# A decoder step on one core: differential heads moved two ahead, their logits in pieces over two PSUM bank pairs, scalings moved to ScalarE, and the first norm put inside the input projection

## The reference, cut to what matters

```
xn  = rmsnorm(x, norm_mix)
qa, ka, va, qi, ki, wi, qb, kb, vb = split(xn @ w_in)      # 2628 columns
qa, ka, qb, kb = rmsnorm over each head of 64              # with their gains
A = attention of qa over the 256 keys chosen by qi, ki, wi # top-k per token
B: for each of 4 heads, causal:
   p_c = softmax(qb_c @ kb_c^T / 8 + bias)   for c = 0, 1
   o   = (p_0 - lam * p_1) @ vb
   out = rmsnorm(o, diff_subln) * (1 - lam_init)
h  = x + concat(A, B) @ w_out
h2 = h + memory attention;   y = h2 + conv FFN
```

## Time and profile before

| | |
|---|---|
| time, median of 3 runs | 2556.97 us (2551.84 to 2562.08) |
| the profiled execution | 2553.21 us, its span 2551.4 us |
| PE busy | 2322.0 us, 91% |
| DVE busy | 1103.8 us, 43% |
| ACT busy | 673.3 us, 26% |
| POOL busy | 678.4 us, 27% |
| first norm | 0 to 33.2 us (start of the first projection matmul); its last square ends at 19.3 us |
| input projection | 33.2 to 418.2 us; a step of 512 columns takes 7.3 us, one of 324 columns 5.7 us |
| differential heads | 418.2 to 593.8 us |
| everything after | 598.3 to 2551.4 us, not touched |

### The profile page before, as it was taken

One profiled execution on the slowest core, in us unless ns is written; L12 is line 12 of the kernel. 1 busy time (PEld: TensorE's weight loads), 2 busy tenths in 40 slices (PEclk: granted clock), 3 DMA queues, 4 the chain that ended last, 5 costly groups with the idle time before them and its releaser, 6 DMA issues. The chain is left out here.

```text
span 2551.4 us, 32464 instructions
## 1 busy us (share of the span) xinstructions
PE 2322.0 (91%) x12441; PEld 1564.4 (61%) x12461; DVE 1103.8 (43%) x2457; ACT 673.3 (26%) x1713; POOL 678.4 (27%) x722
## 2 busy tenths in 40 slices
PE   6999997886888888888889898989999999999999
PEld 4644443563455555555544345458888888888887
DVE  4469997883355443333413112243433433370001
ACT  2321112452455444544501014311111111100000
POOL 1021131112455455567700010021212222201110
PEclk9999998997999999998999899999999999999999
DMA  3211101004699698876730204101111111122221
GB/s 136 73 64 67 47 1 41 1 1 149 222 337 316 240 317 308 299 241 195 202 151 1 82 0 165 66 36 49 36 51 34 51 34 51 34 72 74 71 64 39
DMA packets 148605, 281.74 MB, mean 110 GB/s; under 512 B 14485, under 2 KB 83780, under 8 KB 148452
## 3 DMA queue, kind: packets, MB, share of 16 engines
q0 software_dynamic: 49408, 176.19, 20.6%
q1 hardware_dynamic: 80756, 90.50, 10.7%
q10 hardware_dynamic: 18288, 12.98, 1.7%
HBM read 261.68 MB, written 17.94 MB: 110 GB/s over the span
## 5 line engine op out<-in xcount | busy, mean ns | idle before, releaser
L607 PE MATMUL PS<-region 128*128 128x512 f32 (+5 forms) x864 | 331.7, 539 | 4.3 <-DMA region<-w_in 4.3
L2569 PE MATMUL PS<-region,ffn_w 128*128 128x264 f32 x1408 | 323.3, 389 | 1.6 <-PEq L2020 1.6
L2569 PEld LDWEIGHTS PS<-region,ffn_w 128*128 128x128 f32 x1408 | 269.4, 191 | 48.5 <-issue 2.0
L607 PEld LDWEIGHTS PS<-region 128*128 128x128 f32 (+1 forms) x864 | 155.2, 184 | 166.8 <-issue 140.5
L2569 PE MATMUL PS<-region,side 128*128 128x264 f32 x1056 | 243.3, 387 | 1.6 <-POOL side L2526 1.6
L1801 ACT COPY region<-PS 128x512 f32<-128x512 f32 x352 | 193.0, 593 | 183.8 <-PE PS L1680 90.3
L2569 PEld LDWEIGHTS PS<-region,side 128*128 128x128 f32 x1056 | 198.9, 190 | 35.0 <-POOL side L2526 1.7
L851 DVE TENSOR_SCALAR_CACHE_REDUCE mask<-score,cand 128x384 bf16<-128x384 f32 (+2 forms) x198 | 181.6, 942 | 3.3
L1680 PE MATMUL PS<-ident_f,region 128*128 128x128 f32 x1024 | 141.5, 281 | 23.7 <-ACT region L1801 21.5
L1550 POOL DMA_INDIRECT region<-cache_b_k,gather_b x128 | 121.2, 947 | 138.0 <-PE PS L1680 114.4
L1550 POOL DMA_INDIRECT region<-cache_b_v,gather_b x128 | 122.4, 956 | 90.1 <-PE PS L1763 56.1
(11 more groups left out here) (423 smaller groups left out, 3808.7 us busy)
## 6 DMA issues: line engine op xcount, KB each, us to landing
ffn_w<-w_gate SPq DMA_DIRECT2D x11, 1024.0 KB, 5.4
ffn_w<-w_up SPq DMA_DIRECT2D x11, 1024.0 KB, 5.4
region<-w_in SPq DMA_DIRECT2D x4, 2048.0 KB, 7.8
ffn_w<-w_down ACTq DMA_DIRECT2D x7, 704.0 KB, 5.4
region<-x_prompt ACTq DMA_DIRECT2D x8, 512.0 KB, 7.5
region<-x_prompt SPq DMA_DIRECT2D x8, 512.0 KB, 10.5
mem_keys<-cache_mem_k SPq DMA_DIRECT2D x8, 512.0 KB, 4.2
mem_values<-cache_mem_v SPq DMA_DIRECT2D x8, 512.0 KB, 9.3
```

Of the source, the lines that this page charges most:

```text
L607: last = nc.tensor.matmul(M.PS[0:n, s % 3, 0:chunks[j].width], XT[:, c, t * P:t * P + n], w[j % 2][:, c, 0:chunks[j].width], start=(c == 0 ...
L2569: last = nc.tensor.matmul(M.PS[:, bank, 0:TW], left[:, c, :], right[:, c, :], start=begin and c == 0, stop=(c == KH - 1), skip_group_check ...
```

## The change

1. **First norm inside the projection.** `norm_transpose_stage` becomes a class `FirstNorm` whose parts are called from the projection's block. TensorE turns tiles 0 to 4 before step 0, then one more tile ahead of each of steps 1 to 4; the squares go to PSUM banks 6 and 7, one bank per half tile, not doubled, and the scaled rows to the space of `KTB`. The four pieces of the first weights wait for the scaling of tiles 0 to 3 alone, the second chunk's weights for tile 7.
2. **Scalings of the projection by ScalarE.** In the three chunks with a norm over 512 columns the multiplication by the reciprocal root is done by ScalarE, one activation for each of 8 heads; the keys' gains by GpSimd. `room(s)` counts one VectorE operation there instead of two or three.
3. **Differential heads.** Logits, maxima and exponentials run two heads ahead. Heads of up to 512 keys are one piece, longer ones two pieces of half the keys; piece g uses banks 0-1 or 2-3 (g % 2), one branch in each bank. A maximum takes both branches in one instruction; with two pieces a minimum joins them, and an addition the sums. The output scaling moves from VectorE to ScalarE, without the gain, which becomes a scale of the "M" copy (a column `sub`, loaded by one more transfer of `first_loads`). TensorE's order is `logits(n + 2)`, `transposes(n)`, `values(n - 1)`.

```diff
+    def dve(self, eng, s):                       # FirstNorm
+        if s == 0:
+            self.setup.columns(eng)
+            self.scale(eng, 0)
+        for t in range(self.copied, min(NT, s + self.AHEAD + 1)):     # AHEAD = 4
+            if t + 1 < NT:
+                self.scale(eng, t + 1)
+            for b in range(2):
+                eng.wait_ge(self.tr_done, 2 * t + b + 1)
+                nc.vector.tensor_tensor(M.XT[...], M.PS[:, 6 + b, 0:4 * n] ..., ALU.mult
+                    ).then_inc(self.evac_done, 1)
+    def pe(self, eng, s):
+        for t in range(self.turned, min(NT, s + self.AHEAD + 1)):
+            eng.wait_ge(self.scaled, t + 1)
+            for b in range(2):
+                if t:
+                    eng.wait_ge(self.evac_done, 2 * t - 1 + b)
+                for c in range(4):
+                    last = nc.tensor.transpose(M.PS[:, 6 + b, c * n:(c + 1) * n], ...)
+                last.then_inc(self.tr_done, 1)
+        if s == 0:
+            eng.wait_ge(self.sq_done, NT)
+        if s < NT:
+            eng.wait_ge(self.evac_done, 2 * s + 2)
...
                         for x, first in enumerate(w_first):
+                            if first_norm:
+                                sp.wait_ge(first_norm.scaled, x + 1)
...
+                def normalise(s):                # projection, ScalarE, after the sides of step s
+                    act.wait_ge(rstd_done, normed(s + 1))
+                    for h in range(cols // hd):
+                        last = nc.scalar.activation(dst, M.PS[0:n, s % 3, h * hd:(h + 1) * hd], ACT.Copy,
+                                                    scale=rstd[0:n, s % 2, h:h + 1])
+                    last.then_inc(nat_mul, 1)
...
-                    ops = 2 + (len(c.gains(0, P, 0)) if c.gains else 0)
+                    ops = 1 if by_scalar(s) else 2 + (len(c.gains(0, P, 0)) if c.gains else 0)
...
-        def slot(k, a, b):                       # differential heads
-            return M.PS[:, 2 * k:2 * k + 2, :].rearrange("p b n -> p (b n)")[:, a:b]
+        def pieces(n):
+            nk = (heads[n][0] + 1) * P
+            return [(0, nk)] if nk <= CH else [(0, nk // 2), (nk // 2, nk)]
+        def slot(g, w):
+            return M.PS[:, 2 * (g % 2):2 * (g % 2) + 2, 0:w]
...
+                    for x, (a, b) in enumerate(pieces(n)):
+                        g = piece0[n] + x
+                        if g >= 2:
+                            pe.wait_ge(s_used, 2 * (g - 1))
...
+                for what, n in order:            # ScalarE
+                    if what == "B" and n + 2 < N:
+                        exps(n + 2)
+                    ...copies(n)
+                    if n:
+                        square(n - 1)
+                    if n >= 2:
+                        outputs(n - 2)
...
                                                    ALU.add).then_inc(comb_done, 1)
-                    if n + 1 < N:
-                        maxima(n + 1)
-                    if n:
-                        outputs(n - 1)
+                    if n + 2 < N:
+                        maxima(n + 2)
                     M.top.rounds(link, share)
```

More of the change, by code:

```diff
@@ L403, in dve @@
                                                  K(f"new_mask{g}"), ALU.add))
[L406 to L415, removed]
-            "sq_done", "ms_done", "rstd_done", "scaled", "tr_done", "evac_done"))
[L417 to L482, removed]
-                    for c in range(KC):
-                        last = nc.tensor.transpose(M.PS[:, 2 * (t % 2) + c // 4, (c % 4) * n:(c % 4 + 1) * n],
-                                                   xs[0:n, t % 2, c * P:(c + 1) * P], K("ident")[0:n, 0:n])
-                    last.then_inc(tr_done, 1)
@@ L503, in projection_stage @@
     turned = lambda s: count(s, lambda c: c.sources is not None)
+    counted = lambda s: count(s, lambda c: c.gains is not None)
+    by_scalar = lambda s: bool(beside and chunks[steps[s][0]].norm and chunks[steps[s][0]].norm[0] > 2 * P)
     def stored(s):
@@ L554, in load @@
                         return
+                    if j == 1 and first_norm:
+                        sp.wait_ge(first_norm.scaled, NB)
                     sp.dma_start(w[j % 2][:, :, 0:c.width],
@@ L672, in _ @@
                                             ALU.pow).then_inc(rstd_done, 1)
+                    if c.gains is not None and by_scalar(s):
+                        pool.wait_ge(nat_mul, k)
+                        if s >= 2 and turned(s - 1):
+                            pool.wait_ge(tr_done, turned(s - 1))
+                        if s >= 2 and stored(s - 2):
+                            pool.wait_ge(store_done[s % 2], stored(s - 2))
+                        for dst, a, b in c.gains(t, n, s % 2):
+                            last = nc.gpsimd.tensor_tensor(dst, a, b, ALU.mult)
+                        last.then_inc(nat_done, 1)
             @block.vector
@@ L729, in _ @@
                         side.dve(dve, s, room(s))
-                    if chunks[j].norm:
+                    if chunks[j].norm and not by_scalar(s):
                         normalise(s, k)
@@ L1039, in prompt_differential_stage @@
     N = len(heads)
-    turn_after = {min(B_H * (i + 1) + 1, N - 1): i for i in range(NB - 1)}
+    turn_after = {min(B_H * (i + 1) + 2, N - 1): i for i in range(NB - 1)}
     order = []
@@ L1134, in _ @@
                 logits(0)
+                logits(1)
                 for what, n in order:
-                    if what == "B" and n + 1 < N:
-                        logits(n + 1)
+                    if what == "B" and n + 2 < N:
+                        logits(n + 2)
                     transposes(what, n)
-                    if what == "B":
+                    if what == "B" and n:
+                        values(n - 1)
+                    if what == "B" and n == N - 1:
                         values(n)
```

229 lines of the change are left out of this document (164 added, 65 removed).

## The result

The changed kernel takes 2540.32 us (median of 20 runs, 2530.39 to 2555.25), the one before 2556.91 us (20 runs, 2551.84 to 2565.81): ratio 0.9939, 95% interval 0.9927 to 0.9951, so 0.6% faster. I had forecast 2522, and 2506 to 2540. The direction was right; the gain is 16.6 us where I had some 35 against this median (33.5 in the sum of the parts). The profiled execution took 2537.3 us (span 2535.5), so its difference of 15.9 us to the span before can be taken apart, each stage from one trace.

What follows compares the result with a forecast made beforehand. TensorE (91% busy) was taken to bound, gains coming from its gaps at start, projection end and heads. Gains 9.0 + 1.7 + 13.8 + 6.0 + 3 = 33.5 us from 2553.2 give 2519.7; forecast 2522, range 2506 to 2540.

Steps and rivals of the forecast that it cites:

- First norm: Projection start: TensorE begins step 0 at about 22.6 instead of 33.2; net gain 9.0 us, bounds 5 and 12.
- So it is hidden: Projection start: the first weights' last piece lands by 24, before its matmuls need it at 26, so costs nothing.
- Scalings: Projection: ScalarE's scaling no longer waits behind VectorE's search at the end; gain 1.7 us, bounds 0 and 2.8.
- rival (c): Projection: ScalarE bounds it, its chain exceeding 7.3 us a step, so the kernel gets slower, 2570 us; chance 0.04.
- Heads up to 512 keys: Differential stage, 16 short heads: two ahead leaves no ring of one head; gain 13.8 us, bounds 5 and 20.
- Heads over 512 keys: Differential stage, 16 long heads: a shorter ring, 6.4 against 6.85 us at 1024 keys; gain 6.0 us, bounds 0 and 14.
- the ring: Long heads: second piece's logits, bias, maximum, minimum, four exponentials and hop in a row, 6.4 us at 1024 keys.
- Tail: End of the differential heads: search finished earlier, head 31's exponentials done a head early; gain 3 us, bounds 1 and 5.
- (e): Start and heads: gains come back as waits of short queues, heads gain nothing, 2542 us; chance 0.06.
- (a): Differential heads: running two ahead gives little, long heads staying a ring and short ones waiting on ScalarE; 2536 us; chance 0.16.
- (d): Projection start: weights late or step 0 slow, gain 5 instead of 9, 2526 us; chance 0.68 shared with the forecast.
- (b): Differential heads become TensorE-bound and the start reaches its bound: gain 50 us, 2505 us; chance 0.06.

Runs made afterwards that it cites:

- experiment 5: Changed kernel with only the first norm kept: scalings by VectorE again and the old differential stage; 2548.47 us, ratio 0.9978 to the kernel before.
- Experiments 2: Changed kernel with late turning: TensorE turns a block's mixed outputs after the next head's logits, not before; 2524.86 us, ratio 0.9887 to the kernel before.
- experiment 3: Changed kernel with ScalarE's copies of head n ahead of the exponentials of head n + 2; 2529.08 us, ratio 0.9898 to the kernel before.
- experiment 4: Changed kernel with the rest of the top-k search left out of the differential stage; 2537.98 us, ratio 0.9943 to the kernel before.
- Experiment 10: Late-turning kernel with another order for the last three heads: some ScalarE copies and scaling before exponentials, values earlier; 2526.67 us, ratio 0.9888 to the kernel before.
- experiment 9: Late-turning kernel with the second piece's maximum taken branch by branch, branch 0's exponentials waiting for branch 0 alone; 2522.95 us, ratio 0.9869 to the kernel before.
- experiment 7: Late-turning kernel with heads over 512 keys cut by branch instead of by keys; 2541.8 us, ratio 0.996 to the kernel before.
- 1: Changed kernel with the differential stage of the kernel before; 2545.44 us, ratio 0.9972 to the kernel before.
- 8: Late-turning kernel with long heads cut by branch and values first for the last two heads; 2542.93 us, ratio 0.9965 to the kernel before.
- 11: Late-turning kernel with the maximum split by branch and the new tail order together; 2519.39 us, ratio 0.9851 to the kernel before.
- 6: Late-turning kernel with TensorE making values of heads 29 and 30 ahead of the turnings of 30 and 31; 2535.3 us, ratio 0.9933 to the kernel before.

## Why the prediction was wrong, point by point

**What bounds.** Right: TensorE's gaps at the start, at the projection's end and in the heads were where the change could gain, and, but for the 1.7 us that the clock gave, it gained there alone.

**First norm.** 7.9 for 9.0. The start at 22.6 was right for the turning. Step 0 gave back 2.2 us where I had taken 1.5. Wrong is "So it is hidden": I priced the weights' pieces with the 3 to 4.5 us of before, where they were issued after the other loads of the start, and now they took 7.9 to 11.0. I also looked at the last piece, and TensorE waited for the first: 1.8 us. It lands right behind setup transfers that were issued before it. That those delay it is argued, not tried.

**Scalings.** 2.8 for 1.7, my upper bound. The activations cost what I took, the chain had its slack, rival (c) didn't come, and the block didn't wait for VectorE's last share as I had it: the search ended its share at 405.3, ahead of ScalarE's copies at 405.6. The estimate of 1.9 us for eight activations from the Trainium skill ("ScalarE: Activation LUTs", What ACT_TABLE_LOAD costs) is near the 1.75 of the trace.

**Heads up to 512 keys.** 15.5 for 13.8. Right in kind and nearly in size: 3.26 us a head for heads 4 to 15 where I had 3.3, 2.48 for the first four where I had 2.95. How much of the latter is the clock isn't shown (experiment 5).

**Heads over 512 keys.** -5.8 for +6.0; this is the step that failed. The larger part, 7.2 us, is a wait that the step leaves out altogether: I summed the ring of `logits`, maxima and exponentials, and took "copies no longer standing first" as a pure gain. The same move puts the copies last, behind four exponentials, and the "M" turnings that stand in TensorE's queue ahead of the next logits wait for them, three times at some 2.6 us, and behind the first of the three TensorE also runs at the lower clock for a while. Experiments 2 and 3 show it from both ends. The rest, 4.6 us, is the ring, mis-sized: without the turnings it took 5.29, 5.81, 6.20 and 6.73 us a head against my 5.1, 5.5, 6.0 and 6.4, and the heads before took 5.34, 5.83, 6.37 and 6.85. For 1024 keys 0.16 of the miss is the second piece of logits (1.06 us to the bias for my 0.9), and one gap, 7.01, has the scan of the search in its way (6.59 without the search, in experiment 4). The sign that I had named, long heads that keep 6.85 us or more, came: the three gaps of 1024 keys in the changed kernel are 8.57, 7.00 and 6.59 us.

**Tail.** -2.4 for +3. The scan is gone from it, as forecast, but I did not count that values now run one head later and copies behind exponentials two heads ahead, so three heads' values lie behind the last exponentials. Experiment 10 gives back 3.5, a part of it perhaps by the clock. The 0.5 us that the three parts leave of the stage's loss are in its first column: 5.5 us to the first exponential for 5.0.

**Stages after.** -3.4 for 0. It isn't shown to be an effect of the change. The same unchanged code took 1952.8 to 1968.3 us in the eleven experiments' profiles, with most of the difference arising between 900 and 1290 us. Across the 20 executions of the changed kernel the time follows the mean granted clock: 2530.4 and 2532.4 at 0.975, 2550.3 at 0.967, 2555.3 at 0.964. What makes the clock fall in one execution and not in another stays open.

**Rivals.** (e), the heads gain nothing, gives 2542 and comes nearest in number to 2540, and half in kind: gains were returned as a wait in a queue, though by the long heads, and 6.9 us of the stage stayed. That the number fits owes something to the 3.4 us of the later stages, which no rival had. (a), little gain from two ahead, gives 2536. Its half on long heads is right: with the turning waits gone the ring gives 1.4 us in all (90.7 to 89.4), not 6.0. Its half on short heads is wrong: they gained all that I said. (d) has its share, 1.1 us. (b) and (c) didn't come.

## What to carry to other kernels

When work is moved ahead in one engine's queue, price what it now stands in front of: here a copy behind exponentials made for two heads later held a bank, and TensorE stood at its rarest entry with all else queued behind it. Write out every entry of each queue for one period, the rare ones (every fourth head) and the last periods too. A ring is tested by shortening a link that leaves the instructions of the other engine that could bound as they are (TensorE's in experiment 9); a test that changes the bound's own work, as by branch here, answers another question.

## What the runs showed of the hardware

**Matmuls of 64 rows overlapped here only when they alternated.** 4 matmuls of 64x512 took 1.98 us in one half of the rows and 1.13 when they alternated between the halves (experiment 7). The Trainium skill ("TensorEngine Tiling (Array Packing)", Key Properties) says that different tiles can execute in parallel; the trace agrees, and adds that the order of issue decided.

**The clock in the first steps comes out one of two ways.** Windows from the first step on, of the kernel after and of experiment 3 (columns of the earlier trace rows):

```profile
24.40:29.60 5.20, 5.20 (x24) 3.83 (x24) 1.99 (x8) 0.56 (x4) 0.00 (x0) 1.00 0.08 30
```

```profile
24.40:31.00 6.60, 6.59 (x21) 4.50 (x22) 1.86 (x6) 0.26 (x1) 0.00 (x0) 0.74 0.05 20
```

Both have the same code there, and TensorE had turned tiles, waited for the weights, and was busy without a gap from 24.4 on; step 0 took 4.60 us at 1.00 (2.4 GHz) and 6.29 us in a stretch at 0.74, in part at 1.2 GHz. Four of the profiles (1, 3, 9, 10) had the lower clock, eight not. A second fall, to 0.91 between 80 and 100 us, was there before and in experiments 1, 4, 5, 8, 9, 10 and 11, and not in the kernel after or in 2, 3, 6 and 7: it is the 1.7 us "inside the projection", which is therefore no gain of the change. With the landing of the first weights (23.0 to 24.3) the two move the heads' start from 404.70 (experiment 7) to 409.20 (experiment 9), 4.5 us between kernels that are alike up to it, which is more than some of the edits above are worth. So I compared stages and not times, and for differences of 3 us the parts of a stage.
